# Expert weights in longer runs, and rows that go by token: a change to the MoE stage of a hybrid diffusion layer

## The chip, the core and the metric

The kernel runs on one core of one Trainium2 chip, everything in float32. The time is that of one execution on the device, in microseconds (us), from the first instruction to the last of the core. TensorE does the matmuls; DVE (VectorE), ACT (ScalarE) and POOL (GpSimd) do the element work; SP (SyncE) issues most of the DMAs, and POOL those whose rows are picked by an index. PE stands for TensorE in the profile, SPq for SP's queue.

## What is computed

One layer on 128 context tokens and 512 latent tokens (640 in all, width 1024): modulated RMSNorm, two token mixers (retention, differential attention), gates, an output projection; then modulated RMSNorm and a mixture of experts; a final RMSNorm. The change is in the second half:

```python
h2 = rmsnorm(x, n2) * (1.0 + sc2) + sh2
x = x + g2 * hier_moe(h2, ...)          # then rmsnorm(x, final_norm_g)
# hier_moe: softmax over 4 groups, top 1; softmax over its 8 experts, top 2
w = p_top * e_top / sum(e_top)
combine = einsum('nk,nke->ne', w, one_hot(gidx, 32))
a = silu(einsum('nd,edf->nef', hf, wg)) * einsum('nd,edf->nef', hf, wu)
y = einsum('nef,efd->nd', a * combine[:, :, None], wd)
```

Each of the 32 experts has gate and up weights of 1024 x 256 and down weights of 256 x 1024, 1 MB (1.05e6 bytes) each, about 100 MB for all.

## The kernel before

The tokens are five tiles (t = 0 to 4) of 128. Up to about 1030 us the kernel does modulation, mixers and dense projections; every dense matmul is split into three fp32r products (L860) whose weights (`w_in`, 1 KB runs) SP loads unit by unit (L566). The order of this part is a plan written out in the program, which each engine walks.

**Router.** For tile t DVE writes h2 in two operations (`router_input`, L1575 and L1577), SP stores it to `h2_rows` (L691), TensorE transposes it (L918) and multiplies it with the router weights (L927). DVE then ranks the tokens of every expert in a long chain of small operations (to L1774): token n with its k-th expert gets a place, 64 places an expert, 128 places a pair of experts; places past the 64th go to overflow blocks, of which this data has none. Ten matmuls (L1046) over one-hot places turn this around into `row_idx`, the token of each place (0 where a place is empty), and DVE casts it (L1785). POOL waits for it.

**Expert stage.** 16 pairs of experts. For pair p POOL gathers 128 rows of `h2_rows` (L1928) into one of two buffers; TensorE transposes them (L1053), ACT copies them (L1329), TensorE does the gate-up product (L1059, 32 records), ACT a tanh (L1334), DVE two operations (L1789, L1793, `silu_up`), TensorE transposes (L1065), ACT copies (L1338), TensorE does the down product (L1072). ACT and DVE copy its halves to `y_out` (L1344, L1800; two buffers) and SP stores 128 rows to `y_rows` (L761). The weights have six slots. Experts 0 to 5 are loaded before the stage; afterwards SP, in the order of its queue (`pair_io`), waits for the gate-up of p and loads the gate and up weights of two later experts into those slots (L662), waits for the down product of p and loads the down weights (L665), then waits for y of p and stores it. Pairs 0 and 1 refill for pairs 3 and 4, pair 2 (slots 4 and 5) refills nothing, pair 3 refills for pair 5, and so on; each refill is 6.29e6 bytes.

```python
sp.dma_start(w_gu[slot][:, :, g, :], w[0, e].rearrange("(k p) f -> p k f", p=P))       # L662
sp.dma_start(w_dn[slot], a["moe_w_down"][0, e].rearrange("(k p) n -> p k n", p=P))     # L665
```

With `(k p)` a partition reads eight pieces of 1 KB (gate, up) or two of 4 KB (down).

**Tail.** After the last store SP tells POOL, which gathers for each tile the first and the second row of each token from `y_rows` (L1946, ten gathers). ACT scales the first by its combining weight (L1384), DVE adds the second times its own (L1843), POOL multiplies by the gate g2 (L1951), DVE adds x (L1839), ACT squares and sums (L1391), POOL takes the inverse root (L1915, L1916), DVE scales (L1833), SP stores (L803).

In the first half SP also fills the overflow part of `y_rows` with 5 MB (`fill_out`, L606).

Of the kernel before, what the change touches and what calls it, by code (L numbers as in the profile page):

```python
# [22 lines left out]
F32 = mybir.dt.float32  # L23
# [10 lines left out]
NT = 5  # L34
# [12 lines left out]
NPAIR = (NE + OVER) // 2  # L47
EPS = 1e-6
# [3 lines left out]
def host_constants():  # L52
# [44 lines left out]
def build(nc, a, o, coff, roff, nconst, nroute):  # L97
    ctx = ExitStack()
    with ctx:
# [86 lines left out]
        n2_row = h2[1]  # L186
        assert nroute <= 2 * KB
# [5 lines left out]
        w_gu = [at(k, KC * 2 * FF).rearrange("p (k g f) -> p k g f", k=KC, g=2) for k in (28, 52, 86, 138, 162, 118)]  # L193
# [40 lines left out]
        val_pair = split_at("tokens_by_pair", val_kb, 2 * NT, NPAIR)
        own_pair = scratch(2 * NT * NPAIR).rearrange("p (x n) -> p x n", n=NPAIR)
        ov_cmp = scratch(OVER * NE).rearrange("p (j e) -> p j e", j=OVER)
        ov_f, n_ov_f = scratch(OVER), scratch(1)
        assert scr_at[0] <= 198, scr_at[0]
        row_idx = sb("row_idx", [P, NPAIR], U32)
        idx_now = sb("idx_now", [P, 1], U32)  # L240
        y_idx = sb("y_idx", [P, 2 * NT], U32)
# [27 lines left out]
        y_dram = nc.dram_tensor("y_rows", [SLOTS, D], F32).ap()  # L269
# [208 lines left out]
        for e in plan:  # L478
# [31 lines left out]
        st_fill = sem("st_fill")  # L510
# [8 lines left out]
        ov_take = sem("ov_take")  # L519
# [4 lines left out]
        (ov_free, ov_idx, ov_x, ov_w, ov_xt, ov_xr, ov_gu, ov_tanh, ov_half, ov_act, ov_aT, ov_ar, ov_dn, ov_ya,  # L524
         ov_yd, ov_st, ov_over) = (sem("ov_" + x) for x in ("free", "idx", "x", "w", "xt", "xr", "gu", "tanh", "half",
# [19 lines left out]
        def _(sp):  # L545
# [1435 lines left out]
```

## Time and profile before

| | us |
|---|---|
| median of 3 runs (lowest, highest) | 1404.19 (1401.6, 1406.04) |
| span of the profiled execution | 1407.0 |
| TensorE busy in it | 1167.8 |
| DVE, ACT, POOL busy | 496.5, 406.8, 98.7 |
| mean DMA rate | 166 GB/s |

The profiled execution has no other time than its span, first instruction to last; it lies 2.8 us above the median and 1 us above the highest run. A busy time is the time in which the engine had an instruction in work; for TensorE it counts pipelined matmuls and doesn't mean full speed. The rows further down give, for a stretch, what each engine did in it, and for a wait, who ended it.

### The profile page before, as it was taken

What the parts mean: (1) busy time and instruction counts of PE and PEld (TensorE: products, weight loads), DVE (VectorE), ACT (ScalarE), POOL (GpSimd) and SP (SyncE); (2) the same over time, 40 slices, a digit from 0 to 9 for tenths busy, and PEclk for the clock granted to TensorE, in tenths of its full rate; (3) what the DMA queues carried; (4) which work ended last, traced back from release to release, by engine and by line L of the source; (5) the groups of instructions that cost most, each with busy time, mean ns of one, the idle gap of its engine ahead of it and who ended that gap; (6) DMA issues with size and microseconds to landing.
All of it is one profiled execution on the core that took longest, in us unless ns stands there. A gap on an engine that the chain in (4) does not pass through costs nothing.

```text
span 1407.0 us, 19069 instructions
## 1 busy us (share of the span) xinstructions
PE 1167.8 (83%) x7939; PEld 940.5 (67%) x7939; DVE 496.5 (35%) x895; ACT 406.8 (29%) x878; POOL 98.7 (7%) x102
## 2 busy tenths in 40 slices
PE   2799999989979999999988987999845977777730
PEld 0488899889869999899967777989842322222210
DVE  1511127554334434324354444555552100000007
ACT  3522222122234445432255444222110111111102
POOL 0000001120000000000000000000001000000027
PEclk9899999999999999999999998999966999888975
DMA  8556532114411121232221114733186999999953
GB/s 308 199 197 201 173 90 65 56 38 141 167 60 53 61 90 54 76 100 81 68 65 50 45 46 165 276 96 121 46 288 214 380 368 380 380 376 374 373 186 142
DMA packets 152002, 233.84 MB, mean 166 GB/s; under 512 B 8377, under 2 KB 128994, under 8 KB 148466
## 3 DMA queue, kind: packets, MB, share of 16 engines
q1 hardware_dynamic: 148178, 219.06, 45.5%
q0 software_dynamic: 3744, 13.63, 2.7%
q8 instruction: 59, 0.97, 0.3%
q14 instruction: 21, 0.17, 0.0%
HBM read 206.43 MB, written 26.25 MB: 165 GB/s over the span
## 4 chain that ended last, share of the span: by engine, by line
PE 57%; SPq 14%; DVE 9%; issue 7%; ACT 7%; DMA 4%; POOL 2%; POOLq 0%; DVEq 0%; ACTq 0%
PE ps L860 37%; SPq L662 10%; PE ps L1007 6%; PE ps L1059 3%; PE ps L1036 3%; DMA w_loaded<-in_w_in 3%; SPq L665 3%; ACT arena L1298 2%; PE ps L1072 1%; DVE w_low L1590 1%; PE ps L827 1%; DVE mx L1658 1%; ACT w_high L1271 1%; DVE mx L1659 1%; PE ps L1018 1%
## 5 line engine op out<-in xcount | busy, mean ns | idle before, releaser
L860 PE MATMUL ps<-w_high,h_high 128*128 128x256 f32 x1280 | 371.8, 291 | 12.3 <-DVE arena L1517 7.0
L860 PE MATMUL ps<-w_low,h_high 128*128 128x256 f32 x1280 | 364.7, 285 | 0.0
L860 PE MATMUL ps<-w_high,h_low 128*128 128x256 f32 x1280 | 364.6, 285 | 0.0
L860 PEld LDWEIGHTS ps<-w_high,h_high 128*128 128x128 f32 x1280 | 248.2, 194 | 27.9 <-ACT arena L1241 10.1
L860 PEld LDWEIGHTS ps<-w_low,h_high 128*128 128x128 f32 x1280 | 248.4, 194 | 0.5 <-issue 0.2
L860 PEld LDWEIGHTS ps<-w_high,h_low 128*128 128x128 f32 x1280 | 248.1, 194 | 0.0
L1059 PE MATMUL ps<-arena 128*64 128x512 f32 x512 | 136.9, 696 | 46.6 <-DMA arena<-in_moe_w_up 40.4
L1590 DVE TENSOR_TENSOR w_low<-w_loaded,w_high 128x2048 fp32r<-128x2048 f32 x44 | 100.8, 2291 | 175.3 <-ACT w_high L1271 175.2
L1059 PEld LDWEIGHTS ps<-arena 128*64 128x64 f32 x512 | 42.8, 160 | 139.5 <-issue 139.5
L1241 ACT COPY arena<-ps 128x256 f32<-128x256 f32 x100 | 37.2, 372 | 250.3 <-PE ps L860 250.3
L1298 ACT ACTIVATE arena<-ps,neg_mx 128x768 f32<-128x768 f32 (+1 forms) x80 | 62.8, 790 | 135.9 <-DVE neg_mx L1660 135.9
L1271 ACT CAST w_high<-w_loaded 128x2048 fp32r<-128x2048 f32 x44 | 83.9, 1908 | 60.7 <-DMA w_loaded<-in_w_o 33.6
L1007 PE MATMUL ps<-arena 128*128 128x256 f32 (+2 forms) x288 | 94.7, 470 | 3.2 <-ACT arena L1190 2.0
L1789 DVE SCALAR_TENSOR_TENSOR arena<-arena,ps 128x256 f32<-128x256 f32 x16 | 6.7, 421 | 185.4 <-ACT arena L1334 185.4
L1072 PE MATMUL ps<-arena 128*64 128x512 f32 x256 | 58.5, 598 | 12.3 <-ACT arena L1338 12.3
L1658 DVE TENSOR_REDUCE mx<-ps 128x1 f32<-128x768 f32 (+1 forms) x40 | 32.9, 823 | 98.6 <-PE ps L1007 98.6
L1007 PEld LDWEIGHTS ps<-arena 128*128 128x128 f32 x288 | 51.2, 193 | 23.0 <-issue 15.6
L1036 PE MATMUL ps<-arena 128*128 128x128 f32 x384 | 49.3, 278 | 11.8 <-ACT arena L1305 11.8
L1334 ACT ACTIVATE arena<-ps 128x256 f32<-128x256 f32 x16 | 6.1, 383 | 172.6 <-PE ps L1059 172.6
L1036 PEld LDWEIGHTS ps<-arena 128*128 128x128 f32 x384 | 45.5, 192 | 14.6 <-ACT arena L1305 14.6
L893 PE MATMUL ps<-const,arena 128*128 128x128 f32 x256 | 41.3, 291 | 12.7 <-POOL arena L1910 3.5
L860 PE MATMUL ps<-w_high,m_high 128*128 128x256 f32 x160 | 47.9, 299 | 2.6 <-DVE m_low L1559 0.8
(249 smaller groups left out, 1718.3 us busy)
## 6 DMA issues: line engine op xcount, KB each, us to landing
w_loaded<-in_w_in SPq DMA_DIRECT2D x32, 1024.0 KB, 5.7
arena<-in_moe_w_gate SPq DMA_DIRECT2D x32, 1024.0 KB, 12.1
arena<-in_moe_w_up SPq DMA_DIRECT2D x32, 1024.0 KB, 13.2
arena<-in_moe_w_down SPq DMA_DIRECT2D x32, 1024.0 KB, 12.3
arena<-in_w_ada SPq DMA_DIRECT2D x24, 1024.0 KB, 5.8
y_rows<-arena SPq DMA_DIRECT2D x16, 512.0 KB, 12.2
y_rows<-h_high SPq DMA_DIRECT2D x2, 2560.0 KB, 17.2
gates<-arena SPq DMA_DIRECT2D x40, 128.0 KB, 1.7
```

What stands on the lines that cost most here:

```text
L662: sp.dma_start(w_gu[slot][:, :, g, :], w[0, e].rearrange("(k p) f -> p k f", p=P)).then_inc(ld_gu[slot], 16)
L665: sp.dma_start(w_dn[slot], a["moe_w_down"][0, e].rearrange("(k p) n -> p k n", p=P)).then_inc(ld_dn[slot], 16)
L860: mm = pe.matmul(out[:, 0:N256], x[:, t, k * P:(k + 1) * P], w[i % 2][:, k, :], start=(k == 0 and j == 0), stop=(k == KC - 1 and j == 2))
L893: mm = pe.transpose(out[:, k * P:(k + 1) * P], src[k], ident)
L1007: mm = pe.matmul(score[c][:, lo:hi], q, keys, start=True, stop=True, skip_group_check=True)
L1036: mm = pe.matmul(B(7)[:, 0:P], mixedT[s % 2][:, k * P:(k + 1) * P], v, start=(k == 0), stop=(k == 5))
L1059: mm = pe.matmul(B(bank_at)[BLK * i:BLK * (i + 1), :], xgT[slot][:, k, BLK * i:BLK * (i + 1)], w_gu[e0 + i][:, k, :, :].rearrange("p g f - ...
L1072: mm = pe.matmul(B(5 + n)[BLK * i:BLK * (i + 1), :], act_aT[slot][:, k, BLK * i:BLK * (i + 1)], w_dn[e0 + i][:, k, n * N512:(n + 1) * N512 ...
L1271: act.copy(w_hi[i % 2][:], w_raw[i % 2]).then_inc(w_rounded, 1)
L1298: act.activation(probs[:, c, 0:n], score[c][:, 0:n], ACT.Exp, bias=neg_mx[:, s % 2, c:c + 1], scale=DH ** -0.5, accum_out=den[:, s % 2, c: ...
L1590: dve.tensor_tensor(w_lo[i % 2][:], w_raw[i % 2], w_hi[i % 2][:].bitcast(F32), ALU.subtract).then_inc(w_split, 1)
L1658: dve.tensor_reduce(mx[:, 0:1], score[0][:, 0:n], AXX, ALU.max)
```

## The change

Five things are changed together.

1. The input index of the expert and router weights goes to partitions as `(p k)`: a partition reads 8 consecutive rows (gate, up) or 2 (down), one run of 8 KB each. For the products to stay the same, h2 is written and stored with its columns permuted (column q*8+k to place k*128+q), and the SwiGLU output with its columns permuted in the same way for k = 2.
2. The table now gives for each place the row to gather and the row to write to; empty places get 4096, outside both tensors, and the indirect DMAs have a bounds check that leaves such rows out. `y_rows` holds 2 x 640 rows by token, and the rows of y are scattered to it by POOL. The fill is dropped.
3. The combining weight is put in the table as well (a second table product) and multiplied in at the second SwiGLU operation.
4. The table products run in float32.
5. In the tail POOL loads the first rows plainly and adds the second rows in the DMA; DVE does the gate, the addition of x and the multiplication by the final norm's row, ACT the last scaling.

```diff
-    sp.dma_start(w_gu[slot][:, :, g, :], w[0, e].rearrange("(k p) f -> p k f", p=P))
+    sp.dma_start(w_gu[slot][:, g, :, :], w[0, e].rearrange("(p k) f -> p k f", p=P))
-    sp.dma_start(w_dn[slot], a["moe_w_down"][0, e].rearrange("(k p) n -> p k n", p=P))
+    sp.dma_start(w_dn[slot], a["moe_w_down"][0, e].rearrange("(p k) n -> p k n", p=P))
...
-            def pair_io(p, par, into=None):
...
-                sp.wait_ge(y_a, p + 1)
-                sp.wait_ge(y_d, p + 1)
-                sp.dma_start(y_dram[bass.ds(p * P, P), :], y_out[:, par, :]).then_inc(st_y[par], 16)
+            def next_weights(p, e, slot):
+                sp.wait_ge(pe_gu, p + 1)
+                for i in range(2):
+                    load_gate_up(e + i, slot + i)
+                sp.wait_ge(pe_dn, p + 1)
+                for i in range(2):
+                    load_down(e + i, slot + i)
...
+                mm = pe.matmul(B(5)[:, 0:2 * NPAIR], hot_pos[:, x, :], by_pair[:, x, 0:2, :]...)
+            mm.then_inc(pe_table, 1)
+            pe.wait_ge(route_d, 5)
+            for x in range(2 * NT):
+                mm = pe.matmul(B(7)[:, 0:NPAIR], hot_pos[:, x, :], by_pair[:, x, 2, :], ...)
...
+                by_row = lambda v: v.rearrange("p (q k) -> p q k", k=KC)
+                link(dve.scalar_tensor_tensor(out=rows_of(h2[t % 2]), in0=by_row(x1[:, t, :]), scalar=rstd[:, t:t + 1],
+                                              in1=by_row(scale2[:, i, :]), op0=ALU.mult, op1=ALU.mult))
+                dve.tensor_tensor(rows_of(h2[t % 2]), rows_of(h2[t % 2]), by_row(shift2[:, i, :]), ALU.add)
...
+            dve.tensor_tensor(by_pair[:, :, 0, :], own_pair, over_last(R("from_row"), NPAIR), ALU.mult)
+            dve.tensor_tensor(by_pair[:, :, 1, :], own_pair, over_last(R("to_row"), NPAIR), ALU.mult).then_inc(route_d, 1)
+            dve.tensor_tensor(by_pair[:, :, 2, :], own_pair, over_last(w_tok..., NPAIR), ALU.mult).then_inc(route_d, 1)
+            dve.wait_ge(pe_table, 1)
+            dve.tensor_scalar(row_idx[:], B(5)[:, 0:NPAIR], float(NOWHERE), None, ALU.add)
+            dve.tensor_scalar(to_idx[:], B(5)[:, NPAIR:2 * NPAIR], float(NOWHERE), None, ALU.add).then_inc(idx_ready, 1)
...
+                dve.scalar_tensor_tensor(out=act_a[:, par, :].rearrange("p (k q) -> p q k", k=2), in0=pairs_of(act_s[:, par, :]),
+                                         scalar=w_slot[:, bass.ds(column, 1)], in1=pairs_of(src[:, FF:2 * FF]), ...)
...
+            for t in range(NT):
+                dve.wait_ge(ld_y[t], 32)
+                link(dve.tensor_tensor(y1[:, t, :], y1[:, t, :], g2_rows[:, 1 if t == PT else 0, :], ALU.mult))
+                dve.tensor_tensor(x1[:, t, :], x1[:, t, :], y1[:, t, :], ALU.add).then_inc(x2_ready, 1)
+                dve.wait_ge(x2_ready, t + 1)
+                dve.tensor_tensor(y2[:, t, :], x1[:, t, :], fin_row, ALU.mult).then_inc(fin_scaled, 1)
...
+            def rows_in(p):
+                if p >= 2:
+                    pool.wait_ge(pe_xt, p - 1)
+                pool.indirect_dma_start(xg[:, p % 2, :], None, h2_dram, ...row_idx[:, p:p + 1]...,
+                                        bounds_check=last_row, oob_is_err=False).then_inc(ld_xg[p % 2], 16)
+            def rows_out(p):
+                pool.wait_ge(y_a, p + 1)
+                pool.wait_ge(y_d, p + 1)
+                pool.indirect_dma_start(y_dram, ...to_idx[:, p:p + 1]..., y_out[:, p % 2, :], None,
+                                        bounds_check=last_place, oob_is_err=False).then_inc(st_y[p % 2], 16)
+            rows_in(0)
+            rows_in(1)
+            for p in range(PAIRS):
+                if p + 2 < PAIRS:
+                    rows_in(p + 2)
+                rows_out(p)
...
             for t in range(NT):
+                pool.dma_start(y1[:, t, :], y_dram[t * P:(t + 1) * P, :]).then_inc(ld_y[t], 16)
             for t in range(NT):
+                pool.wait_ge(ld_y[t], 16)
+                pool.dma_start(y1[:, t, :], y_dram[(NT + t) * P:(NT + t + 1) * P, :], accum_op=ALU.add).then_inc(ld_y[t], 16)
```

## Rows read from the trace of the kernel before

**Rows 1.** The page: busy time of TensorE; GB/s moved in 40 slices.

```profile
PE 1167.8 (83%) x7939; PEld 940.5 (67%) x7939; DVE 496.5 (35%) x895; ACT 406.8 (29%) x878; POOL 98.7 (7%) x102
...
GB/s 308 199 197 201 173 90 65 56 38 141 167 60 53 61 90 54 76 100 81 68 65 50 45 46 165 276 96 121 46 288 214 380 368 380 380 376 374 373 186 142
```

**Rows 2.** Waits, 1142 to 1299 us: total us, times, longest us.

```profile
PE ps L1059 <- DMA arena<-in_moe_w_up: 34.8, 8, 6.3
```

**Rows 3.** Windows: us, busy us of PE, PEld, DVE, ACT, POOL, clock, DMA share, GB/s.

```profile
30.00:35.00 5.00, 3.87 (x16) 0.40 (x16) 2.07 (x10) 4.85 (x11) 1.38 (x2) 1.00 1.01 421
40.00:45.00 5.00, 3.08 (x18) 2.17 (x19) 3.27 (x10) 1.48 (x1) 0.00 (x0) 0.77 1.12 354
345.00:355.00 10.00, 10.00 (x86) 10.00 (x85) 5.17 (x8) 3.33 (x5) 0.00 (x0) 1.00 1.06 432
1081.89:1339.50 257.61, 194.91 (x838) 69.57 (x838) 23.00 (x45) 34.78 (x75) 12.18 (x13) 0.90 1.06 373
1142.65:1298.50 155.85, 113.77 (x462) 39.63 (x464) 11.58 (x23) 17.96 (x39) 7.49 (x8) 0.86 1.07 376
1326.00:1331.00 5.00, 4.00 (x24) 1.70 (x20) 0.84 (x2) 1.73 (x4) 0.00 (x0) 1.00 1.09 356
1336.00:1341.00 5.00, 1.44 (x4) 0.53 (x6) 0.00 (x0) 0.00 (x0) 0.00 (x0) 0.88 1.05 401
```

**Rows 4.** Chain of work that ended last: start us, us, what.

```profile
1064.74 4.55 DMA arena<-h_rows,row_idx
...
1142.65 6.72 SPq L662
...
1298.50 7.48 SPq L662
...
1355.09 4.31 DMA y_rows<-arena
```

**Rows 5.** Timeline of TensorE, three gate-ups: start us, us; idle before.

```profile
1113.78 7.04 PE L1059 MATMUL ps<-arena 128*64 128x512 f32 x32
...
1146.61 9.78 PE L1059 MATMUL ps<-arena 128*64 128x512 f32 x32 [6.29 <-DMA arena<-in_moe_w_up]
...
1339.56 8.78 PE L1059 MATMUL ps<-arena 128*64 128x512 f32 x32 [4.95 <-issue]
```

**Rows 6.** Groups of DVE by form: busy us, mean ns.

```profile
L1575 DVE SCALAR_TENSOR_TENSOR arena<-arena,rstd 128x1024 f32<-128x1024 f32 x5 | 6.4, 1283 | 9.3 <-POOL rstd L1916 9.2
...
L1577 DVE TENSOR_TENSOR arena<-arena 128x1024 f32<-128x1024 f32 x5 | 6.1, 1225 | 0.2
...
L1457 DVE COPY modc<-ps 128x32 f32<-128x32 f32 x3 | 0.6, 192 | 2.7 <-PE ps L836 2.7
...
L1774 DVE TENSOR_TENSOR tokens_by_pair<-arena 128x130 fp32r<-128x130 f32 x2 | 0.5, 292 | 0.0
...
L1772 DVE TENSOR_TENSOR arena<-arena 128x260 f32<-128x260 f32 x1 | 0.4, 430 | 0.0
```

**Rows 7.** Waits, 1000 to 1407 us.

```profile
PE ps L918 <- DVE arena L1577: 5.5, 2, 3.0
```

**Rows 8.** Timeline of TensorE, router: logits and table.

```profile
1037.17 3.63 PE L927 MATMUL ps<-arena 128*128 128x36 f32 x16 [1.16 <-ACT arena L1266]
...
1061.84 2.31 PE L1046 MATMUL ps<-tokens_by_pair,hot_places 128*128 128x26 f32 x10 [12.42 <-DVE tokens_by_pair L1774]
```

**Rows 9.** Gathers on line 1928, issue to landing.

```profile
DMA to landing us min/median/max: 4.6/7.3/9.0
```

**Rows 10.** Timeline of SP, POOL and DVE in the tail.

```profile
1355.09 0.33 SPq L761 DMA_DIRECT2D y_rows<-arena  x1
...
1361.08 0.94 POOL L1946 DMA_INDIRECT arena<-y_rows,y_idx  x1 [65.66 <-SPq L799]
...
1362.32 0.94 POOL L1946 DMA_INDIRECT arena<-y_rows,y_idx  x1 [0.31 <-issue]
...
1399.03 1.21 DVE L1839 TENSOR_TENSOR arena<-arena 128x1024 f32<-128x1024 f32 x1
```

More of the change, by code:

```diff
@@ L523, in build @@
         st_y = [sem("st_y0"), sem("st_y1")]
[L524 to L526 removed]
+        (ov_free, ov_idx, ov_x, ov_w, ov_xt, ov_xr, ov_gu, ov_tanh, ov_half, ov_act, ov_aT, ov_ar, ov_dn, ov_y,
+         ov_st) = (sem("ov_" + x) for x in ("free", "idx", "x", "w", "xt", "xr", "gu", "tanh", "half",
+                                   "act", "aT", "ar", "dn", "y", "st"))
         ld_y = [sem(f"ld_y{t}") for t in range(NT)]
[L528 to L530 removed]
+        ov_take = sem("ov_take")
+        x2_ready, fin_sq, fin_rstd, fin_ready, ld_fin = (sem(x) for x in ("x2_ready", "fin_sq", "fin_rstd", "fin_ready", "ld_fin"))
+        fin_scaled = sem("fin_scaled")
+        st_fin = sem("st_fin")
         n_freed = {"A": count["A"], "D": count["D"]}
@@ L600, in mod_out @@
                              a["state_ret_fwd"][0, 0].rearrange("h d e -> d h e")).then_inc(ld_state, 16)
-            def fill_out():
-                for i in range(OVER * BLK // (NT * P)):
-                    r0 = NE * BLK + i * NT * P
-                    sp.dma_start(y_dram[r0:r0 + NT * P, :].rearrange("(p k) n -> p (k n)", k=NT),
-                                 left["h"][1][:].bitcast(F32).rearrange("p t n -> p (t n)")).then_inc(st_fill, 16)
             def state_out_dma(i):
@@ L1245, in high_part @@
                 wait_freed(act, where[("T4", what, t, half)])
-                if what == "o" and t == 0 and half == 0:
-                    act.wait_ge(st_fill, 16 * 2)
                 c = slice(N512 * half, N512 * (half + 1))
@@ L1376, in _ @@
                         act.wait_ge(ov_dn, j + 1)
-                        act.copy(y_out[:, 0, 0:N512], B(5)).then_inc(ov_ya, 1)
+                        act.copy(y_out[:, 0, 0:N512], B(5)).then_inc(ov_y, 1)
                     with act.Else():
@@ L1783, in _, with silu_up @@
             link(dve.tensor_copy(n_ov[:], over_end[:, NE - 1:NE]))
-            dve.wait_ge(pe_table, 1)
-            dve.tensor_copy(row_idx[:], B(5)[:, 0:NPAIR]).then_inc(idx_ready, 1)
-            def silu_up(src, par, wait, done):
+            def silu_up(src, par, wait, done, column):
                 ins = dve.scalar_tensor_tensor(out=act_s[:, par, :], in0=act_t[:, par, :], scalar=1.0, in1=src[:, 0:FF],
@@ L1792, in silu_up @@
                 dve.wait_ge(wait[0], wait[1])
-                dve.scalar_tensor_tensor(out=act_a[:, par, :], in0=act_s[:, par, :], scalar=0.5, in1=src[:, FF:2 * FF],
+                pairs_of = lambda v: v.rearrange("p (q k) -> p q k", k=2)
+                dve.scalar_tensor_tensor(out=act_a[:, par, :].rearrange("p (k q) -> p q k", k=2), in0=pairs_of(act_s[:, par, :]),
+                                         scalar=w_slot[:, bass.ds(column, 1)], in1=pairs_of(src[:, FF:2 * FF]),
                                          op0=ALU.mult, op1=ALU.mult).then_inc(done, 1)
```

189 lines of the change are left out of this document (76 added, 113 removed).

## The prediction, made before the changed kernel was run

> **What bounds the kernel now.** I read the slices of the page first, then the waits, then windows of the expert stage. From about 1090 us on the core moves 360 to 380 GB/s, as nowhere else for so long [rows 1]. From 1142 to 1299 us TensorE waits for expert weights before each pair of experts, 34.8 us in 8 waits [rows 2], and the transfers fill their share (1.07) at 376 GB/s [rows 3]. One `up` load of a refill is issued at 1142.65 and its counterpart eight pairs on at 1298.50 [rows 4]: a period of 155.85 / 8 = 19.48 us. Less 34.8 / 8 = 4.35 us of waiting, TensorE needs 15.1 us of it. TensorE's busy share of 83% [rows 1] is thus no bound here; bytes over transfer rate are.
>
> The rate depends on the run length [rows 3]. `w_ada` (8 KB runs) moves at 421 GB/s; where `w_in` (1 KB runs) is in the queue it is 354. At the end of the expert stage, with only gate and up weights (1 KB runs) left, it is 356, and 401 with the down weights (4 KB runs). I take 354, 401 and 421. Check by bytes up to the last pair's gate-up: 26 of 32 experts are loaded from 1081.9 us on; by then 54.5 MB of gate/up and 26 MB of down weights have landed, and 16.2 MB of rows (14 gathers and 14 stores of 0.524 MB, 1.5 MB of broadcasts). 54.5/0.354 + 26/0.401 + 16.2/0.401 = 154 + 65 + 40 = 259 us. The trace has 257.7 (1081.9 to 1339.56) [rows 3, 5]. The three rates hold, so I use them for after.
>
> **Parts 1 and 2, weights in 8 KB runs, empty places skipped.** 640 tokens take two places each: 1280 of 2048 rows. A gather or store shrinks from 0.524 to 0.328 MB on average; 28 of them lose 5.5 MB. After: 54.5 + 26 = 80.5 MB of weights and 16.2 - 5.5 = 10.7 MB of rows, 80.5/0.421 + 10.7/0.401 = 191 + 27 = 218 us. A pair then needs 6.29/0.421 + 0.655/0.401 = 16.6 us, still above TensorE's 15.1. Before the refill for pair 5 the queue runs dry: all earlier transfers end by about 1119, and this refill waits for a gate-up that ends at 1113.78 + 7.04 = 1120.8 now [rows 5] and 2.5 later after (part 4). With the time from issue to first bytes I add 3 us: 221 against 257.7, **-36.7 us**. The clock: gate-up takes 7.04 us without a wait ahead of it, 9.78 us after one of 6.29 [rows 5]; the granted clock of 1142 to 1299 is 0.86 of 2.4 GHz on average [rows 3], a mix of that level and 1.2 GHz. Waits shrink, so I expect no loss there, and the 15.1 us hold such slow starts already.
>
> **Part 3, order inside the vectors.** Both h2 operations of a tile (1.28 and 1.23 us) now write with steps of 512 B. A transposing copy of 32 elements takes 192 ns, 130 elements in order take 292, 260 take 430 [rows 6]: about 1.05 ns an element all along, no surcharge for the transposed read. I take 0. The other end is double: TensorE waits for h2 twice as it is, 5.5 us in all [rows 7], and pays 2.5 us more each time; the other three tiles have cover by dense work, and if part of it is gone 2 us more: +5 to +7. No row gives reason for a gain. The second SwiGLU operation (256 elements, about 0.43) gets the same step and a column instead of 0.5: +0 to 0.4 us a pair, hidden by the 1.5 us that TensorE has to spare, and at most 0.4 for the last pair.
>
> **Part 4, router table.** Two products of 130 elements (0.29 each) become two of 260 (0.43): +0.3. One cast goes and one comes: 0. The 10 table matmuls took 2.31 us in fp32r; in fp32, 8 products of a router tile took 3.63, 0.45 each, and at the same speed 10 cost 4.5: +2.2 [rows 6, 8]. Sum **+2.5 us** before the first gather; bounds 0 (the 2.31 stays) and 5 (twice that surcharge, for 52 columns against 36). The third product, the second table (4.5 us) and the overflow list move behind the index. They lie beside the first gather (4.55 us, [rows 4]) and a gate-up of 7 to 9 us. Without that cover they would cost about 7 us, once.
>
> **Part 5, scatters on POOL's queue.** POOL now issues gather p+2, waits for y of p, then scatters. Behind that wait stands gather p+3, which needs the transposes of p+2, later still: nothing is delayed. An indirect transfer keeps POOL 0.94 + 0.31 us [rows 10], two per pair 2.5 of 16.6 us. SP loses its y wait and carries weights alone. The buffer of p is wanted two pairs on, 33 us, against landings of 4.6 to 9.0 us [rows 9]. The last store is on the path: from 1355.09 to POOL's first gather 1361.08 are 6.0 us, of which the store is 4.31 [rows 4, 10]. A scatter takes between 4.31 and 9.0; I take 5.3 (the nearest row, a gather of 4.55 with little beside it, and some for the way out to memory), 0.3 to start and 1.7 for the branch as now: 7.3, **+1.3 us**.
>
> **Part 6, the tail.** Before: from 1361.08 to the span's end at 1407.0, 45.9 us. After: five plain loads on POOL, five adding loads, then three DVE operations a tile. Neither kind of load is in the trace. Issue lies between SP's 0.33 and 1.25 us of POOL's indirect ones [rows 10], landing between 4.31 and 9.0. I take 1.25 and 5.3, the queue being the same. First adding load issued at 5 x 1.25 = 6.2, landed at 12.5, with 1 us for reading its destination. DVE per tile 3 x 1.21 + gaps = 3.8, with no POOL multiply beside it; the fifth addition is done at 12.5 + 4 x 3.8 + 2.5 = 30.2. From the last addition's end (1399.03 + 1.21) to 1407.0 are 6.8 us now [rows 10]; ACT's scaling takes the place of DVE's there. Sum 37.0, **-8.9 us**. Adding loads up to 3.8 us apart stay hidden; at 6 us apart the gain is gone. Other end: all loads fast, DVE alone, -14.
>
> The dropped 5 MB fill at 342 us: 0. TensorE is busy for 10.00 of 10 us beside it [rows 3]; the fill would cost only if TensorE waited there.
>
> **Sum.** -36.7 + 2.5 + 1.3 - 8.9 = -41.8 us. The profiled execution has a span of 1407.0 us, so 1365 for it; the median of the runs is 1404.2, 2.8 below that span. Forecast 1404.2 - 41.8 = **1362 us**.
>
> **Rivals.** (A) The rate doesn't rise with the run length, only the bytes fall: 91.2 MB at the 373 GB/s of the whole stretch [rows 3] are 245 us, +24 on the forecast, 1386. For: with writes beside, memory could be the limit. Against: 421 and 432 GB/s elsewhere [rows 3]. Chance 0.10. The Trainium skill ("DMA: Bandwidth & Descriptors", Specifications) has full line rate from 512 B on, by which 1 KB runs lose nothing and this rival holds; the trace disagrees, with 354 against 421 GB/s. (B) Steps of 512 B double DVE's operations: +6, 1368. For: only a small copy speaks against it. Chance 0.20. The Trainium skill ("Advanced Engine Details and Errata", SBUF Cachelines) says that accesses which each touch another 16-byte line pay a penalty, which would be this rival. No row here steps so through a vector. (C) Adding loads land 6 to 7 us apart: +10, 1372, 0.10. (D) It doesn't skip; empty places still move: 5.5/0.401 = 14 us, 1376, 0.05. (E) Slower than before: skipping is decided row by row in POOL's queue, and an indirect transfer holds POOL for X instead of 0.94 us. X decides once 2X passes 16.6, and makes the kernel slower than before once 13 refills x (2X - 16.6) exceed 41.8, at X = 9.9. At X = 11: 13 x 5.4 = 70, 1432. For: no row shows such a check, nor a scatter. Against: ten times the 0.94 of now. Chance 0.05.
>
> **Chances.** Forecast 0.50 (own range 1352 to 1370), B 0.20, A 0.10, C 0.10, D 0.05, E 0.05. Within 0.3%, about 4 us, is what a measurement of this kernel can't tell from no change: 0.02, half out of E and half out of A. Faster 0.94, slower 0.04. The range goes down by the tail's and the router's other ends and up to B, C and D: 1346 to 1380; A and E are left out.
>
> **What would show it.** Right: windows of the expert stage at 410 GB/s or more, refills 16.6 us apart, TensorE's waits for weights under 2.5 us each, indirect transfers near 0.94 us on POOL, h2 operations still 1.28 and 1.23, about 37 us from the first y load to the end. Wrong: still 376 GB/s (A), h2 operations of 2.5 us (B), DVE waiting for each adding load (C), 7.3 MB a pair (D), POOL busy all through the stage (E).

## The result, and the profile after

The changed kernel takes 1372.35 us in the median of six runs (1364.4 to 1374.81), the kernel before 1406.32 in six runs beside it: a ratio of 0.974, 95% interval 0.970 to 0.977 (the ratio is not taken from the medians; theirs is 0.976). The forecast was 1362, its range 1346 to 1380. The measured gain is 34 us where the sum said 41.8. One of the four executions of k8, further down, took 1728.76 us at a mean granted clock of 0.649 (0.939 to 0.947 in the others) and is left out of its numbers. The profiled execution of after is one of its two quickest: 1365.45 us, of which the span is 1363.5. The same kernel, profiled again in the first experiment, has a span of 1374.3. So I read both and keep them apart.

The page of after: GB/s in 40 slices, and the DMA packets (90273; the kernel before made 152002). Before it was 368 to 380 GB/s over the expert stage [rows 1].

```profile
GB/s 308 215 184 204 200 94 62 62 39 49 115 48 58 65 69 79 63 111 68 76 87 47 47 22 34 356 139 105 78 62 385 164 402 421 421 420 421 420 95 222
DMA packets 90273, 222.28 MB, mean 163 GB/s; under 512 B 9881, under 2 KB 64962, under 8 KB 74706
```

Windows of after (columns as in [rows 3]): the first refill to the last gate-up, the middle of that, its last 7 us, and where the 5 MB fill used to be.

```profile
1078.34:1303.96 225.62, 183.29 (x839) 67.18 (x839) 26.63 (x45) 36.21 (x75) 28.25 (x28) 0.95 0.99 407
1142.00:1290.00 148.00, 115.59 (x512) 41.48 (x510) 15.97 (x27) 21.73 (x45) 17.21 (x17) 0.93 1.02 421
1297.00:1303.96 6.96, 4.00 (x19) 1.20 (x19) 0.69 (x1) 1.24 (x3) 0.89 (x1) 1.00 0.43 182
...
345.00:355.00 10.00, 10.00 (x86) 10.00 (x85) 5.23 (x9) 3.32 (x5) 0.00 (x0) 1.00 0.30 93
```

The first line answers to 257.61 us at 373 GB/s. The third says what the sum didn't have: in the last 7 us before the last gate-up the transfers are down to 182 GB/s, where before they ran at 401 [rows 3]. Most parts of the loads have landed by then; the last gate-up waits for the few that haven't, as the semaphores show below.

Waits of after, 1142 to 1299 us (34.8 us in 8 before, [rows 2]), and the chain of work that ended last, from 1228 us on.

```profile
PE ps L1042 <- DMA arena<-in_moe_w_up: 19.7, 9, 4.0
```
```profile
1227.80 0.33 SPq L652
1228.23 0.38 SPq L652
...
1229.23 24.22 DMA arena<-in_moe_w_up
...
1253.68 7.11 PE ps L1042 x32
...
1262.38 25.45 DMA arena<-in_moe_w_up
...
1288.06 7.11 PE ps L1042 x32
...
1297.80 3.65 PE ps L1055 x16
1301.46 2.50 issue
1303.96 8.80 PE ps L1042 x32
...
1322.08 3.21 DMA y_rows<-arena,to_idx
```

Two things differ from [rows 4]. The issue of a 1 MB load held SP's queue for 6.72 and 7.48 us and now takes 0.33 to 0.38; and the chain has become a loop: a gate-up ends, its slots are refilled, the refill lands 24 to 25 us later, and the gate-up two pairs on can start.

In the chain's last steps, 1288.06 to 1303.96, the profile shows no transfer, and it puts the 2.50 us before the last gate-up down to "issue", time in which it sees no wait. That is misleading, and much hangs on it. The program waits there (`ld_gu`) for the gate and up loads of the last two experts. A load raises its semaphore (the counter on which an engine waits) 16 times, as parts of it land, and the traces keep the time of every rise. The gate and up loads of the last expert make 32 rises, from 1289.29 to 1303.86; the gate-up starts at 1303.96. In all twelve profiled executions the last gate-up starts 0.09 or 0.10 us after the last of these rises. So the last gate-up waits for weights as the others do, and what counts is the part of a load that lands last.

Groups of DVE by form; TensorE's transposes of h2 by form; the router table and the second table on TensorE; the scatters' line.

```profile
L1781 DVE SCALAR_TENSOR_TENSOR arena<-arena,ps 128x256 f32<-128x256 f32 x16 | 10.6, 663 | 2.2 <-DVE arena L1776 2.2
L1558 DVE SCALAR_TENSOR_TENSOR arena<-arena,rstd 128x1024 f32<-128x1024 f32 x5 | 10.1, 2020 | 10.0 <-POOL rstd L1890 9.9
L1560 DVE TENSOR_TENSOR arena<-arena 128x1024 f32<-128x1024 f32 x5 | 9.7, 1936 | 0.2
L1776 DVE SCALAR_TENSOR_TENSOR arena<-arena,ps 128x256 f32<-128x256 f32 x16 | 6.7, 421 | 143.6 <-ACT arena L1315 143.6
```
```profile
L896 PE MATMUL ps<-const,arena 128*128 128x128 f32 x40 | 7.2, 337 | 9.6 <-DVE arena L1560 9.6
```
```profile
1056.39 4.51 PE L1024 MATMUL ps<-arena 128*128 128x52 f32 x20 [12.48 <-DVE arena L1757]
1060.70 4.43 PE L1029 MATMUL ps<-arena 128*128 128x26 f32 x20
```
```profile
L1910 POOL DMA_INDIRECT y_rows<-arena,to_idx x16: 968/1007/1013, 1086.1 to 1322.1; - x16
...
DMA to landing us min/median/max: 3.2/8.3/9.0
```

The h2 operations are 1.57 times as long as before [rows 6] (2020 for 1283 ns, 1936 for 1225), the second SwiGLU operation (L1781) takes 663 ns beside 421 for the first, and TensorE waits 9.6 us for h2 in all, 5.5 before.

The tail of after on POOL and on DVE (start us, us; idle before).

```profile
1322.08 0.97 POOL L1910 DMA_INDIRECT y_rows<-arena,to_idx  x1 [18.03 <-DVE arena L1789]
1326.90 2.73 POOL L1943 DMA_DIRECT2D arena<-y_rows  x5 [3.85 <-issue]
1331.35 0.91 POOL L1946 DMA_DIRECT2D arena<-y_rows  x1 [1.72 <-DMA arena<-y_rows]
```
```profile
1339.84 1.23 DVE L1822 TENSOR_TENSOR arena<-arena 128x1024 f32<-128x1024 f32 x1 [18.52 <-DMA arena<-y_rows]
...
1343.51 1.22 DVE L1822 TENSOR_TENSOR arena<-arena 128x1024 f32<-128x1024 f32 x1
```

DVE starts 12.9 us after the first load of y (1326.90 to 1339.84) and then takes 3.65 us a tile without a wait.

The stages of every profiled execution, read off the timelines (us; each column from the end of the one before it; "casts": start of the last of the weight casts that follow each other every 14.4 us on ACT; "first gate-up" and "last gate-up" are their starts, and what lies between them is called the stage below; the last column is the span):

| kernel | casts | logits done | first gate-up | last gate-up | last down ends | first load of y | end | span |
|---|---|---|---|---|---|---|---|---|
| before | 697.0 | 343.8 | 31.8 | 266.9 | 14.7 | 6.8 | 45.9 | 1407.0 |
| after | 688.8 | 346.5 | 34.5 | 234.2 | 16.6 | 6.3 | 36.6 | 1363.5 |
| after again (k1) | 691.7 | 352.1 | 34.6 | 236.4 | 16.8 | 6.3 | 36.5 | 1374.3 |
| TensorE reads in steps (k2) | 689.1 | 341.2 | 34.8 | 235.3 | 13.3 | 6.3 | 36.7 | 1356.7 |
| short runs (k3) | 688.7 | 342.9 | 34.5 | 262.2 | 14.9 | 6.3 | 36.7 | 1386.2 |
| fill back (k4) | 695.4 | 352.0 | 34.5 | 236.2 | 13.4 | 6.3 | 36.6 | 1374.3 |
| full gathers (k5) | 695.2 | 348.3 | 34.8 | 235.5 | 15.1 | 6.3 | 36.8 | 1372.0 |
| k2, mixed tail (k6) | 690.7 | 345.6 | 34.9 | 234.9 | 15.0 | 6.3 | 31.9 | 1359.2 |
| before, 8 KB runs alone (k7) | 692.8 | 345.4 | 31.8 | 240.9 | 13.1 | 7.0 | 46.0 | 1376.9 |
| k2, nothing skipped (k8) | 692.2 | 345.4 | 35.1 | 239.0 | 14.9 | 6.4 | 36.8 | 1369.7 |
| k2, gathers skip all (k9) | 691.7 | 345.7 | 34.7 | 223.1 | 15.0 | 6.3 | 36.7 | 1353.2 |
| k3, nothing skipped (k10) | 688.6 | 345.9 | 35.3 | 267.6 | 16.6 | 6.4 | 36.7 | 1397.1 |

### The profile page after: what moved, and what is told of

Its sections match the earlier page's. It is cut to its first block and busy times, and to the rows that moved or that the text cites. A ratio compares the mean times of both kernels' runs of the same rounds, so it can differ in the third digit from the quotient of the medians.

```text
span 1363.5 us, 19120 instructions
## 1 busy us (share of the span) xinstructions
PE 1155.2 (85%) x7969; PEld 936.6 (69%) x7969; DVE 500.0 (37%) x899; ACT 408.1 (30%) x878; POOL 101.3 (7%) x113
## 2 busy tenths in 40 slices
DMA packets 90273, 222.28 MB, mean 163 GB/s; under 512 B 9881, under 2 KB 64962, under 8 KB 74706
## 5 line engine op out<-in xcount | busy, mean ns | idle before, releaser
L1042 PE MATMUL ps<-arena 128*64 128x512 f32 x512 | 124.8, 644 | 23.5 <-DMA arena<-in_moe_w_up 19.7
L1641 DVE TENSOR_REDUCE mx<-ps 128x1 f32<-128x768 f32 (+1 forms) x40 | 32.9, 823 | 96.9 <-PE ps L985 96.9
L1055 PE MATMUL ps<-arena 128*64 128x512 f32 x256 | 60.0, 611 | 9.8 <-ACT arena L1319 9.8
L1014 PEld LDWEIGHTS ps<-arena 128*128 128x128 f32 x384 | 45.5, 192 | 14.6 <-ACT arena L1286 14.6
L838 PE MATMUL ps<-w_high,od_high 128*128 128x256 f32 x160 | 46.3, 289 | 1.7 <-DVE od_whole L1470 0.9
## 6 DMA issues: line engine op xcount, KB each, us to landing
arena<-in_x_sample SPq DMA_DIRECT2D x8, 512.0 KB, 10.8
```

Source lines behind the costliest of these rows:

```text
L838: mm = pe.matmul(out[:, 0:N256], x[:, t, k * P:(k + 1) * P], w[i % 2][:, k, :], start=(k == 0 and j == 0), stop=(k == KC - 1 and j == 2))
L1014: mm = pe.matmul(B(7)[:, 0:P], mixedT[s % 2][:, k * P:(k + 1) * P], v, start=(k == 0), stop=(k == 5))
L1042: mm = pe.matmul(B(bank_at)[BLK * i:BLK * (i + 1), :].rearrange("p (g f) -> p g f", g=2), xgT[slot][:, k, BLK * i:BLK * (i + 1)], w_gu[e0 ...
L1055: mm = pe.matmul(B(5 + n)[BLK * i:BLK * (i + 1), :], act_aT[slot][:, k, BLK * i:BLK * (i + 1)], w_dn[e0 + i][:, k, n * N512:(n + 1) * N512 ...
L1641: dve.tensor_reduce(mx[:, 0:1], score[0][:, 0:n], AXX, ALU.max)
```

## The experiments

Each was timed beside the kernel before on its own chip. Medians are over its runs; the ratio to before leaves the profiled execution out. The stages above are of the profiled execution.

**k1, the kernel after once more**, with no edit: how far do two profiled executions of it lie apart, and where?

> The changed kernel itself, again. Its six runs lie at 1364 to 1365 (two) and 1372 to 1375 us (four), while its profile is of a run at 1365.5. If the 8 us between come from where the TensorE clock happens to fall in the dense part (theory 1), the profile shows the same expert stage (first gate-up to last gate-up 234 us, refills 16.9 us apart) and the same tail (36.6 us), and the difference lies before 1000 us. If they come from the expert stage itself (theory 2: TensorE and transfers are nearly level there, and an extra slow gate-up makes TensorE the later one), a profile at 1372 has 240 us or more between first and last gate-up.

Measured: median 1373.08 us, ratio 0.973 (0.969 to 0.977). The 10.8 us between the two spans are 2.9 in the dense part, 5.6 up to the logits and 2.2 in the expert stage; the other parts agree within 0.2. The middle of the stage moves at 420 GB/s in both. So the quick execution of after is luck of the parts before the stage, and the 34 us of the medians, not the 43.5 of the two spans, are the change's. Over the last 37 to 40 us up to the logits TensorE's granted clock is 0.81 in the quick execution and 0.69 in this one:

```profile
998.50:1035.30 36.80, 26.82 (x186) 25.05 (x184) 19.05 (x16) 7.43 (x14) 2.19 (x6) 0.81 0.46 184
```
```profile
1003.70:1043.80 40.10, 31.52 (x186) 29.93 (x184) 19.11 (x16) 7.43 (x14) 2.20 (x6) 0.69 0.45 179
```

**k2, the order taken by TensorE's reads**: DVE writes in order, the transposes read with steps.

```diff
-    pe.transpose(..., h2[t % 2][:, k * P:(k + 1) * P], ident)
+    pe.transpose(..., h2[t % 2].rearrange("p (q k) -> p k q", k=KC)[:, k, :], ident)
...
-    dve.tensor_tensor(rows_of(h2[t % 2]), rows_of(h2[t % 2]), by_row(shift2[:, i, :]), ALU.add)
+    dve.tensor_tensor(h2[t % 2], h2[t % 2], shift2[:, i, :], ALU.add)
```

(the same for the gathered rows and the SwiGLU output).

> The reordering is taken off DVE: h2 and the SwiGLU output are written in order, and TensorE's transposes read every 8th (every 2nd) column instead. Weights, rows, table and tail as in the changed kernel. Theory S (the steps of 512 B cost DVE 0.74 + 0.71 us a tile and 0.24 us a pair): h2 operations back to 1.28 and 1.23 us, the waits of TensorE for h2 from 9.6 to about 5.5 us, total 3 to 5 us less than the changed kernel. Rival: the steps only move; the 8 transposes of a tile take 1.5 times their 1.09 us or more, 16 gathers and 5 tiles of them, and the time stays or grows by 5 us.

Measured: median 1364.81, ratio 0.970 (0.967 to 0.973), 8.3 us under k1 on the same chip. The groups of k2 by form, DVE and TensorE:

```profile
L1779 DVE SCALAR_TENSOR_TENSOR arena<-arena,ps 128x256 f32<-128x256 f32 x16 | 7.7, 481 | 2.2 <-DVE arena L1775 2.2
L1557 DVE SCALAR_TENSOR_TENSOR arena<-arena,rstd 128x1024 f32<-128x1024 f32 x5 | 6.4, 1283 | 9.3 <-POOL rstd L1888 9.2
L1559 DVE TENSOR_TENSOR arena<-arena 128x1024 f32<-128x1024 f32 x5 | 6.1, 1225 | 0.2
```
```profile
L896 PE MATMUL ps<-const,arena 128*128 128x128 f32 x40 | 7.1, 337 | 5.5 <-DVE arena L1559 5.5
```

The DVE operations have their old 1283 and 1225 ns back, and the same 40 transposes take 337 ns each whether they read in order (after) or in steps of 32 bytes: for h2 the permutation costs nothing on TensorE and much on DVE. The two other permutations cost TensorE a little: in k2 the 8 transposes of a pair's gathered rows take 1.16 us (1.09 in after), and the two of the SwiGLU output 0.50 (0.44), while DVE's second SwiGLU operation falls from 663 to 481 ns. The stage shows neither (235.3 us; 234.2 and 236.4 in after and k1). From the cast of the first column of the stages to the logits, the four executions with DVE steps take 346.5, 352.1, 352.0 and 348.3 us (mean 349.7; after, k1, k4, k5), the other eight 341.2 to 345.9 (mean 344.5): 5.2 us by the stages, 8 by the medians. The waits for h2 give about 3 of it (8.0 to 9.6 us in the four, 4.8 to 5.5 in the others); the rest I put down to the clock of that stretch, which none of the runs holds fixed.

**k3, the weights in 1 KB and 4 KB runs again**, natural order everywhere, the rest of the change kept.

```diff
-    w[0, e].rearrange("(p k) f -> p k f", p=P)
+    w[0, e].rearrange("(k p) f -> p k f", p=P)
```

> The 8 KB runs alone are undone: expert and router weights are loaded in runs of 1 KB and 4 KB again and all vectors keep their order; skipped places, table, scatters and tail stay. Theory R (run length sets the rate): windows of the expert stage at 370 to 376 GB/s, the stretch from first refill to last gate-up from 226 to about 248 us (54.5 MB/0.354 + 26 MB/0.401 + 10.7 MB/0.401 = 246), the h2 steps give back 3 to 5 us: 15 to 20 us more than the changed kernel in all. Rival A (only the bytes count): the rate stays at 420 and the time falls by the 3 to 5 us of the steps.

Measured: median 1392.88, ratio 0.990 (0.987 to 0.993). Against k2, which differs in the run length and in TensorE's order of reading, 28 us and 262.2 against 235.3 us of stage. Against before, skipping has taken only 4.7 us off the stage.

**k4, the 5 MB fill back** at its old place in SP's queue.

```diff
+    for i in range(OVER * BLK // (NT * P)):
+        sp.dma_start(fill_dram[r0:r0 + NT * P, :]..., left["h"][1]...).then_inc(st_fill, 16)
```

> The fill of 5 MB is put back at its old place (into a tensor of its own, with ACT's wait for it later on); all else as in the changed kernel. In the profiles the stretch from the 16th to the 18th weight cast on ACT took 34.7 us before and 31.2 after. Theory F (the weight load of the next unit lies behind the fill in SP's queue and TensorE waits for it): this stretch is 34 to 35 us again, and the total 3 to 4 us more. Rival (chance of the clock): the stretch stays near 31 us, or differs among kernels without the fill as much.

Measured: median 1380.26, ratio 0.980 (0.977 to 0.983), 7 us over k1. ACT's weight casts of k4 and then of after, around the fill (start us, us):

```profile
348.73 1.90 ACT L1260 CAST w_high<-w_loaded 128x2048 fp32r<-128x2048 f32 x1
365.79 1.91 ACT L1260 CAST w_high<-w_loaded 128x2048 fp32r<-128x2048 f32 x1 [2.55 <-DMA w_loaded<-in_w_in]
383.49 1.91 ACT L1260 CAST w_high<-w_loaded 128x2048 fp32r<-128x2048 f32 x1
```
```profile
345.71 1.89 ACT L1252 CAST w_high<-w_loaded 128x2048 fp32r<-128x2048 f32 x1
360.11 1.89 ACT L1252 CAST w_high<-w_loaded 128x2048 fp32r<-128x2048 f32 x1
376.87 1.92 ACT L1252 CAST w_high<-w_loaded 128x2048 fp32r<-128x2048 f32 x1
```

34.8 us with the fill against 31.2 without: the next unit of weights lies behind it in the queue and lands late. All nine executions without the fill have 31.2 there. Of the two other kernels with it, before has 34.7 and k7 32.9. Behind the fill, at 365 to 375 us, the granted clock is 0.83 in k4 and in before and 1.00 in k7 and after: the late weights alone cost 1.7 us (k7), and with the lower clock behind them 3.6, which k4 still has at the end of the dense part (695.4 us, k1 691.7). The other 3.4 of the 7 are not explained; the four runs of k1 lie 11.5 us apart.

**k5, full gathers**: an empty place fetches row 0 again; the scatter still skips.

```diff
-    r["from_row"] = token - NOWHERE
+    r["from_row"] = token * 1.0
-            dve.tensor_scalar(row_idx[:], B(5)[:, 0:NPAIR], float(NOWHERE), None, ALU.add)
+            dve.tensor_scalar(row_idx[:], B(5)[:, 0:NPAIR], 0.0, None, ALU.add)
```

> The kernel after, except that the gather no longer skips: an empty place fetches row 0 again, as before the change. The scatter still skips, so y is the same. The gathers move 2.75 MB more (14 of them, 0.2 MB each). Theory B (bytes count, the term of the prediction): 2.75 MB at 0.401 MB/us = 6.9 us more between first and last gate-up, 241 us instead of 234 to 236, and a median near 1380 against 1373. Rival P (an empty place costs its packets whether or not it moves bytes; the trace of after has 144 packets for every indirect transfer): the stage stays within 2 us of 236, median within 3 us of 1373. Rival T (TensorE, not the weights, ends last in the stage now): also within 2 us, but then the rate rises above 421 GB/s without the waits for weights growing beyond 20 us.

Measured: median 1374.29, ratio 0.977 (0.973 to 0.981); stage 235.5 us, like after and k1 (234.2, 236.4). The 2.5 MB more between the first refill and the last gate-up cost next to nothing: the mean rate rises from 407 to 416 GB/s, as the queue now stays full to within 1 us of the last gate-up, instead of 7. Time and waits (19.4 us) fit rivals P and T alike. k9 rules out P, and the semaphores rule out T, by which TensorE would end last: here too the last gate-up starts 0.09 us after the last part of its weights has landed. The added bytes went beside parts of the loads that had been early anyway (table under k8).

```profile
1087.08:1313.83 226.75, 185.13 (x839) 67.69 (x839) 26.65 (x45) 36.21 (x75) 27.87 (x28) 0.94 1.01 416
```

**k6, a mixed tail on top of k2**: tiles 0 and 1 load both rows plainly and DVE adds them, tiles 2 to 4 keep the adding loads.

```diff
+                if t < PLAIN:
+                    pool.dma_start(y2[:, t, :], y_dram[(NT + t) * P:(NT + t + 1) * P, :]).then_inc(ld_y[t], 16)
...
+                if t < PLAIN:
+                    link(dve.tensor_tensor(y1[:, t, :], y1[:, t, :], y2[:, t, :], ALU.add))
```

> The kernel k2_pe_reads_steps (order taken by TensorE's reads, no 512 B steps on DVE), and in the tail tiles 0 and 1 load both rows plainly and DVE adds them; tiles 2 to 4 keep the adding loads. Theory L (the tail of after is the latency of two loads behind each other, 12.9 us from the first y load to DVE's first operation, then DVE at 3.65 us a tile): tile 0 needs two plain loads in parallel, DVE starts at about 6 to 7 us instead of 12.9, two tiles cost 1.2 us more each, the adding loads of tiles 2 to 4 have landed by then (issued at about 6, landed by 15): DVE is done at 6.5 + 2 x 4.9 + 3 x 3.65 + ... , the tail takes 36.6 - 6.4 + 2.4 = 32 to 33 us and the median is 1361 against 1365 of k2. Rival W (the adding loads become the bound, since they start later and land 2.5 us apart or more): tail 35 to 37 us, no gain.

Measured: median 1361.31, ratio 0.968 (0.964 to 0.972), the fastest of all kernels that compute the whole layer; the interval overlaps that of k2, and it is the trace that tells the two apart. DVE and POOL in its tail:

```profile
1332.73 1.22 DVE L1822 TENSOR_TENSOR arena<-arena 128x1024 f32<-128x1024 f32 x1 [11.03 <-DMA arena<-y_rows]
...
1342.87 1.22 DVE L1823 TENSOR_TENSOR arena<-arena 128x1024 f32<-128x1024 f32 x1 [0.22 <-DMA arena<-y_rows]
```
```profile
1327.30 0.59 POOL L1944 DMA_DIRECT2D arena<-y_rows  x1 [3.85 <-issue]
...
1337.21 0.92 POOL L1949 DMA_DIRECT2D arena<-y_rows  x1 [6.10 <-DMA arena<-y_rows]
```

DVE starts 5.4 us after the first load instead of 12.9, and waits 0.22 us once for the first adding load: the tail is 31.9 us for 36.7, against 32 to 33 expected. The tail of after was two loads in a row and then DVE; its adding loads as such were not too slow.

**k7, the kernel before with the 8 KB runs alone** (order by TensorE's reads as in k2; rows, table, stores and tail as before).

```diff
-    sp.dma_start(w_gu[slot][:, :, g, :], w[0, e].rearrange("(k p) f -> p k f", p=P))
+    sp.dma_start(w_gu[slot][:, g, :, :], w[0, e].rearrange("(p k) f -> p k f", p=P))
```

> The kernel before with part 1 alone: expert and router weights to partitions as (p k), one 8 KB run each, and TensorE reads h2, the gathered rows and the SwiGLU output in the matching order, so DVE has no steps of 512 B. Rows are not skipped, table, scatter and tail are as before. Theory of the prediction: 80.5/0.421 + 16.2/0.401 + 3 = 235 us instead of 257.7 from the first refill to the last gate-up, -23 us, median near 1385, and skipping would be worth the other 14 us. Rival P (skipping is worth 5 us only, as in the kernel with short runs): the 8 KB runs alone give -27 or -28 us, median 1379 to 1381, stage 239 to 240 us between first and last gate-up against 266.9. Rival T (TensorE ends last once the runs are long, so that skipping on top adds nothing): -30 us or more, median 1377 or less.

Measured: median 1379.22, ratio 0.981 (0.976 to 0.986); stage 240.9 us, 26 less than before. The run length, with TensorE's reads in the matching order, gives 28 of the 34 us. The chain of k7 no longer lies on SP's issue instructions (0.33 and 0.38 us each).

```profile
1080.06:1310.89 230.83, 186.13 (x838) 70.83 (x839) 23.01 (x45) 34.78 (x75) 12.17 (x13) 0.95 1.01 417
1142.00:1290.00 148.00, 114.32 (x504) 42.93 (x502) 13.11 (x26) 20.28 (x44) 7.49 (x8) 0.93 1.02 423
```

**k8, k2 with nothing skipped**: empty places gather row 0 and write rows of their own behind the 1280.

```diff
+            link(dve.scalar_tensor_tensor(out=B(5)[:, NPAIR:NPAIR + 16], in0=R("x128")[:, 9:25], scalar=R("to_row")[:, 0:1],
+                                          in1=B(5)[:, NPAIR:NPAIR + 16], op0=ALU.add, op1=ALU.min))
```

> The kernel k2_pe_reads_steps, but nothing is skipped: an empty place gathers row 0, and its row of y goes to a place of its own behind the 1280 rows (y_rows is longer by 2048 rows); one DVE operation of 16 elements more before the index. Everything else of the change stays, the scatter on POOL's queue too. It splits the 5.6 us by which the stage of k2 (first to last gate-up, 235.3 us) is shorter than that of k7 (240.9, 8 KB runs alone, rows by SP's store). Theory E (bytes count as predicted, and the skipped ones are partly lost because TensorE, not a weight, is last at the stage's end): the same bytes as k7, so 240 to 242 us, median 5 to 6 above k2, near 1370. Rival Q (it is the store's place on POOL's queue that helps, not the bytes): 235 to 237 us, median within 3 us of k2.

Measured: median 1368.04, ratio 0.972 (0.968 to 0.977), 3.2 us over k2; stage 239.0. So of the 5.6 us between k7 and k2, the bytes are 3.7 and the way of the store up to 1.9, which is near what two executions differ by. Windows of k8 and of k2: first refill to last gate-up, and the last 6.5 us of that.

```profile
1081.05:1311.61 230.56, 188.97 (x839) 71.56 (x839) 23.90 (x45) 34.89 (x75) 28.35 (x28) 0.94 1.01 418
1305.00:1311.61 6.61, 3.66 (x17) 1.10 (x17) 0.69 (x1) 0.77 (x2) 0.99 (x1) 1.00 1.01 421
```
```profile
1074.52:1300.46 225.94, 182.97 (x838) 70.14 (x839) 23.92 (x45) 34.95 (x75) 28.43 (x28) 0.97 0.99 406
...
1294.00:1300.46 6.46, 3.65 (x16) 1.09 (x17) 0.69 (x1) 0.73 (x2) 0.99 (x1) 1.00 0.37 156
```

This is the place where the saving goes. In windows of 1 us, the rate falls below 330 GB/s 234.5 us after the first refill in k8 and 219.0 in k2: by the rate, skipping ends the loads 15.5 us sooner. But the last gate-up comes only 4.6 us sooner (230.6 to 225.9). The semaphore rises tell why. The 16 rises of one down load lie 1.5 to 3.0 us apart in k8 all through the stage; in k2 3.2 us at 1112 us and 12.6 at 1290. For the gate and up loads of the last expert, in us after the first refill:

| kernel | rows skipped | first of 32 rises | last of 32 | last gate-up |
|---|---|---|---|---|
| k7 | none | 225.0 | 230.7 | 230.8 |
| k8 | none | 225.9 | 230.5 | 230.6 |
| k5 | empty places in scatters | 217.8 | 226.7 | 226.8 |
| after | empty places in both | 210.9 | 225.5 | 225.6 |
| k2 | empty places in both | 211.4 | 225.9 | 225.9 |
| k9 | in scatters; gathers from pair 2 on wholly | 204.6 | 213.5 | 213.6 |

From k8 to k2 the first part lands 14.5 us sooner and the last one 4.6 us. The skipped bytes are taken off some parts of the loads and hardly off the slowest, for which TensorE waits. Which parts those are the traces don't tell. It fits that the table fills the 64 places of each expert from the first on: the empty ones are always the last, and a place is a partition. No run spread the empty places in another way, so this last step is argued and not shown.

**k9, k2 with gathers that skip every place from pair 2 on**. The rows of pairs 2 to 15 are left out of the computation.

```diff
+            dve.tensor_scalar(row_idx[:, 2:NPAIR], B(5)[:, 2:NPAIR], 0.0, float(NOWHERE), ALU.mult, ALU.add)
```

> The kernel k2_pe_reads_steps, but from pair 2 on the gathers skip every place: the buffer keeps the rows of pair 0 or 1. The rows of the other pairs are left out of the computation, so y is another. 14 gathers move nothing, 4.4 MB less than in k2 (14 x 0.315 MB). Theory E (weights are last in the middle of the stage, TensorE at its end): between pairs 6 and 14 the period falls from 16.95 us by 0.315/0.421 = 0.75 to about 16.2, and the stage by 6 us, to about 229; the queue is down to a trickle more than 9 us before the last gate-up. Rival P (a skipped place costs about as much as a moved one, 144 packets a transfer either way): 235 us, no change. Rival B (all bytes count up to the last gate-up): 4.4/0.421 = 10.5 us, 225.

Measured: median 1351.70, ratio 0.961 (0.957 to 0.965); stage 223.1 us, 12.2 less than k2. That rules out that a skipped place costs like a moved one, but no theory had the size. I expected 229 and an early end of the loads; they run to the end, and the gain is more than the 10.5 us of the bytes. Window of k9, the last 5 us before its last gate-up:

```profile
1290.00:1295.18 5.18, 2.74 (x14) 0.74 (x11) 0.69 (x1) 0.59 (x1) 0.82 (x1) 1.00 0.93 387
```

The loop of the chain shortens (refills land after 21.2 to 22.9 us instead of 24.3 to 25.5, from the second of the loop on), and TensorE waits 14.8 us instead of 23.7 by the profile. From k8 to k2 4.6 MB go and from k2 to k9 another 4.2 (rate times length of the three windows), for 3.7 and 12.2 us of stage. A gather that skips every place spares all parts of a load alike, and so from k2 to k9 the last part lands 12.4 us sooner, the first only 6.8. Together, from k8 to k9, the first part moves by 21.3 us, about the 8.8 / 0.421 = 20.9 that the bytes give, and the last by 17.0.

**k10, k3 with nothing skipped**: the same with short runs.

> The kernel k3_short_runs with nothing skipped, as in k8. It splits the 4.7 us between before (266.9 us from first to last gate-up) and k3 (262.2) the same way where 1 KB runs keep the weights late to the last pair. Theory E by bytes at 0.373 MB/us: skipping moves 5.1 MB less, so this kernel should take 262.2 + 13.7 = 276 us, which means that rows on POOL's queue cost 9 us there, median near 1405. Rival Q2 (skipping is worth little with short runs too, since the rate falls with the packets): 264 to 267 us, like before, median 1395 to 1398.

Measured: median 1401.99, ratio 0.997 (0.995 to 0.999); stage 267.6, like the 266.9 of before, so that rows on POOL's queue cost nothing there. Theory E missed by 8 us. Windows of k10 and of k3, first refill to last gate-up:

```profile
1078.20:1337.41 259.21, 197.85 (x839) 70.19 (x839) 23.91 (x45) 34.95 (x75) 27.92 (x28) 0.89 1.06 372
```
```profile
1074.20:1328.30 254.10, 195.63 (x844) 70.03 (x840) 23.92 (x45) 34.96 (x75) 28.43 (x28) 0.91 1.04 360
```

Skipping takes off 5.1 us and the rate falls from 372 to 360 GB/s, with the queue full to the end in both (410 and 408 GB/s in the last 2 us). With short runs the chain lies on SP's issue instructions of 3 to 8 us, which the rows, on another queue, don't lengthen much. That is what the chain of before shows too [rows 4]; that it is the reason was not tried by itself.

## Why the prediction was right, and where it wasn't

The forecast of 1362 was 10 us low, the sign and the range right. By steps, the two spans and what single parts gave:

| step | predicted | before to after | before to k1 |
|---|---|---|---|
| dense part (of this the fill up to 3.6) | 0 | -8.2 | -5.3 |
| up to the logits (order inside the vectors) | 0 | +2.7 | +8.3 |
| table and first gather | +2.5 | +2.6 | +2.8 |
| stage (weights, skipping) | -36.7 | -32.7 | -30.6 |
| last pair | 0 | +1.9 | +2.0 |
| last scatter | +1.3 | -0.5 | -0.5 |
| tail | -8.9 | -9.3 | -9.5 |
| sum | -41.8 | -43.5 | -32.7 |

**Part 3 failed.** It was put at 0, with +5 to +7 as its other end. The row it was argued from, a transposing copy of 32 elements, does not carry over: 1024 elements written 512 bytes apart cost 1.57 times as much, not 1.0 and not 2. Rival B was right in direction and in price, 5 to 8 us (stages, medians) against 6, though not in its doubling, and its 1368 was nearer to the 1372 than the forecast. The Trainium skill ("Advanced Engine Details and Errata", SBUF Cachelines) spoke against this change, and the h2 groups and k2 bear it out. It should have weighed more than a row of another size.

**Parts 1 and 2 were near in their sum and wrong in their split.** The rates were right: 421 GB/s for the middle of the stage, as taken from `w_ada`. Rival A, by which it would have stayed at 373, is out, and with it, here, the rule of the Trainium skill ("DMA: Bandwidth & Descriptors", Specifications) of full rate from 512 B on: k3 against k2 has 360 against 406 GB/s over the same rows.

By the prediction's terms the run length was to give 23 us and the skipping 13.7; measured, in the stage, 26.0 (k7) and 3.7 (k8 to k2). The step that failed is "16.2 - 5.5 = 10.7 MB of rows" over a rate: it takes the skipped bytes off the loads as a whole. By the mean rate that held, since the transfers of after fall off 218.7 us after the first refill and the sum had 221. But a load counts only when its last part has landed. That part came at 225.5, and the last gate-up with it at 225.6. The 23 were low, since rows beside long runs don't move at 401 but with the rest (k7 has 417 over all). That the two errors partly cancel is luck. TensorE's own need was not the limit: 16.9 us from gate-up to gate-up (1152.62 to 1288.06, eight pairs) less 2.3 of waiting are 14.6, and in k9 the pairs follow 15.6 to 16.3 us apart from the eighth on.

**Fill, 0**: wrong by 1.7 to 3.6 us in our favour (k7, k4). I had read that TensorE was busy for all 10 us beside it. The cost came some 15 us later, when the weights behind the fill in SP's queue were due: for a transfer one must look at who is queued behind it, not at who works beside it.

**Part 4, +2.5**: 10.79 us from the table to the first gate-up became 13.35 (k1 13.51). The fp32 table takes 4.51 us, 4.5 predicted, and the rest of the table hides where it was said to.

**Part 5, +1.3**: the scatter landed in 3.21 us, not 5.3, quicker than the 4.31 of the store it replaces [rows 10]; the path got 0.5 us shorter. I took the gather as the nearest row; the bound of 4.31 was no lower end either. POOL's scatters take 1.01 us where an indirect transfer took 0.94, so rival E never came near.

**Part 6, -8.9**: right with errors that cancel. The plain loads issue at 0.55 us, not 1.25, so the first adding load waits for a landing and goes out after 4.45 us instead of 6.2; it then takes 8.40 us and not 6.3. DVE starts at 12.94 (12.5 predicted) and takes 3.65 us a tile (3.8). Rival C is out: DVE waits for no later tile.

**Last pair, +1.9**: not in the sum. The last gate-up takes 8.80 us in after, 7.10 in k2 and 8.79 in k10, and from kernel to kernel this stretch varies from 13.1 to 16.8 us: 16.6 and 16.8 in after and k1, 13.4 in k4, which has the same program from there on. I take it for chance of the clock and not for the change.

Rival D is out too: from the first refill to the last gate-up after moves 91.8 MB (0.407 x 225.62), and k8, which skips nothing, 96.4 (0.418 x 230.56).

## What to carry to other kernels

A load is there when its last part is. Before adding up bytes saved, ask whether they come off every part of it: with rows skipped unevenly the first part landed 14.5 us sooner and the last 4.6. Look at the rises of the semaphore as well as at the mean rate. Where the profile says "issue" just before an instruction for which the program has a wait, compare its start with that semaphore. A permutation that one engine must do should go to the one that pays least for it: in TensorE's reads of h2 it was free, in DVE's writes it cost a factor of 1.57. And a chain that lies on issue instructions of several us was here a sign of runs that are too short: with 8 KB runs it was gone (k7).

## What the runs showed that I had not expected

- The issue of a 1 MB load in 1 KB runs holds SP's queue for 6.7 to 7.9 us once in every refill (and most others 2.7 to 3.8 us in the chain of before, where 1.05 MB in 2.87 us are 365 GB/s); in 8 KB runs 0.33 to 0.40 us in the chain of after.
- Skipped places still make packets: over eight pairs in the middle of the stage POOL's queue has 2304 for 16 indirect transfers, 144 each, whether the gathers skip (after) or not (k5). For a skipped place the packet holds 4 bytes where a row's has 4096, and they are cheap: gathers that skip everything made the stage 12.2 us shorter (k9).
- In after the adding loads land 8.4 to 12.5 us after their issue where the plain ones of the same 0.5 MB take 4.2 to 7.9; in k6, with three adding loads behind seven plain ones, they take 5.6 to 8.1. The five of after were issued 1.2 to 2.0 us apart, without a wait of DVE after the first.
- The "issue" time before the last gate-up (2.50 us in after, 4.95 before [rows 5], 1.24 in k7) is in all twelve profiled executions the wait for the last expert's weights.
